# Index scores woven into a unit's products, own places for four query units, smaller first loads from two queues

## The reference

```python
h = rms_norm(x, norm_g)
proj = h @ w_in            # q, k, v, gate_a, u_b, gate_b, q_idx, k_idx, w_idx, merge
q, k = rope(rms_norm(q)), rope(rms_norm(k)); q_idx, k_idx = rope(q_idx), rope(k_idx)
s = einsum('bqhd,bkd->bqhk', q_idx, k_idx)               # index scores, 8 heads
score = einsum('bqhk,bqh->bqk', relu(s), w_idx * scale)
sel = top_k(where(visible, score, -inf), 128)            # keys each query may see
attn = softmax over the selected keys of q k^T, times v
y_a = (attn * silu(gate_a)) @ w_a;  y_b = (pool(u_b) * silu(gate_b)) @ w_b
x = x + (sigmoid(m_a) * y_a + sigmoid(m_b) * y_b) @ w_out
```

## Time and profile before

| | |
|---|---|
| median of 3 runs | 1560.16 us (1555.54, 1560.16, 1560.35) |
| the profiled execution | 1556.19 us, span 1554.3 us |
| PE busy | 1499.2 us, 96% |
| PEld, DVE, ACT, POOL busy | 1208.8, 952.0, 550.9, 971.3 us |
| mean granted TensorE clock | 0.994 |
| read from HBM | 116.02 MB, 76 GB/s over the span |

### The profile page before, as it was taken

The page is one execution under the profiler, slowest core; times in us unless marked ns, Lnnn a source line. Parts: engine busy times, 40 slices in busy tenths (PEclk is TensorE's granted clock), DMA queues, the critical chain, the costliest instruction groups (busy, mean ns, idle before and its releaser), DMA issues.

```text
span 1554.3 us, 24339 instructions
## 1 busy us (share of the span) xinstructions
PE 1499.2 (96%) x8516; PEld 1208.8 (78%) x8516; DVE 952.0 (61%) x2033; ACT 550.9 (35%) x1280; POOL 971.3 (62%) x1496
## 2 busy tenths in 40 slices
PE   7999999999999999999999999999998999999999
PEld 7776547678778778877989888889996877777777
DVE  6874781567676640046777788944448789894251
ACT  4446682333333310044564333341125523333100
POOL 6533415656565688776886644546888774455685
PEclk9999999999999999999999999999999999999999
DMA  7210001222222332332222211112222221121223
GB/s 257 66 48 28 28 1 46 77 71 93 93 94 94 94 104 88 96 98 77 89 69 82 69 55 55 55 55 76 95 82 70 87 88 49 48 68 55 68 95 108
DMA packets 37774, 119.42 MB, mean 77 GB/s; under 512 B 5424, under 2 KB 7600, under 8 KB 37424
## 3 DMA queue, kind: packets, MB, share of 16 engines
q1 hardware_dynamic: 36544, 116.06, 23.3%
q10 hardware_dynamic: 1136, 2.09, 0.4%
HBM read 116.02 MB, written 2.10 MB: 76 GB/s over the span
## 4 chain that ended last, share of the span: by engine, by line
PE 79%; DVE 11%; ACT 3%; POOL 3%; issue 3%; DMA 1%; SPq 0%; POOLq 0%; ACTq 0%; DVEq 0%
PE ps L778 62%; PE ps L1240 3%; PE ps L797 2%; PE ps L791 2%; PE ps L980 2%; PE ps L902 2%; POOL wlo L645 2%; PE ps L1315 1%; DVE score L2385 1%; POOL whi L641 1%; DVE score L2384 1%; PE ps L1310 1%; ACT pts L1539 1%; DVE probs L2403 1%; PE ps L1290 1%
## 5 line engine op out<-in xcount | busy, mean ns | idle before, releaser
L778 PE MATMUL ps<-hh,whi 128*128 128x512 f32 (+1 forms) x1448 | 511.4, 353 | 5.3 <-DVE hl L2177 1.7
L778 PE MATMUL ps<-hl,whi 128*128 128x512 f32 (+1 forms) x1448 | 502.8, 347 | 0.0
L778 PE MATMUL ps<-hh,wlo 128*128 128x512 f32 (+1 forms) x1448 | 501.5, 346 | 0.0
L641 POOL TENSOR_SCALAR whi<-raw 128x256 fp32r<-128x256 f32 x564 | 257.8, 485 | 332.9 <-PE ps L778 331.4
L645 POOL TENSOR_TENSOR wlo<-raw,whi 128x256 fp32r<-128x256 f32 x564 | 442.7, 816 | 11.8
L778 PEld LDWEIGHTS ps<-hh,whi 128*128 128x128 f32 x1448 | 273.9, 189 | 59.4 <-issue 11.3
L778 PEld LDWEIGHTS ps<-hh,wlo 128*128 128x128 f32 x1448 | 274.1, 189 | 34.9
L778 PEld LDWEIGHTS ps<-hl,whi 128*128 128x128 f32 x1448 | 274.0, 189 | 33.0 <-issue 0.7
L735 POOL TENSOR_TENSOR wlo<-raw,whi 128x256 fp32r<-128x256 f32 x160 | 134.7, 873 | 92.8 <-ACT whi L1586 92.8
L1959 DVE TENSOR_TENSOR tmp<-tmp 128x512 f32<-128x512 f32 x12 | 10.8, 900 | 118.3 <-ACT tmp L1624 90.0
L778 PE MATMUL ps<-plain_high,whi 128*128 128x264 f32 (+2 forms) x232 | 74.0, 319 | 6.6 <-POOL wlo L645 6.2
(11 more groups left out here) (363 smaller groups left out, 2709.9 us busy)
## 6 DMA issues: line engine op xcount, KB each, us to landing
raw<-in_w SPq DMA_DIRECT2D x197, 512.0 KB, 3.5
raw<-in_w SPq DMA_DIRECT2D x8, 256.0 KB, 3.4
x<-in_x SPq DMA_DIRECT2D x4, 512.0 KB, 8.1
out<-x SPq DMA_DIRECT2D x8, 256.0 KB, 4.4
raw<-in_w SPq DMA_DIRECT2D x12, 128.0 KB, 2.9
raw<-in_w SPq DMA_DIRECT2D x4, 384.0 KB, 3.4
cw_k<-in_cw1k SPq DMA_DIRECT2D x1, 1024.0 KB, 5.5
cw_v<-in_cw1v SPq DMA_DIRECT2D x1, 1024.0 KB, 7.4
```

The source lines that it names most:

```text
L641: ins = pool.tensor_scalar(whi[s][:, c:c + PIECE], raw[s][:, c:c + PIECE], 1.0, 0.0, ALU.mult, ALU.add)
L778: mm = pe.matmul(out, lhs, rhs, start=start and n == 0, stop=stop and n == 2)
```

## The change

1. `lunit` takes a list `between` of index calls: the first goes ahead of the unit, the others into its matmul stream at equal distances. In a slot with index scores the last unit is taken out of the spacers and computed so, behind the rest; ACT does the relus before that unit's eviction. In the first hybrid layer mg8 moves from slot 10 to slot 9, in the second mg6 from slot 6 to slot 5; the order of units stays.
2. `QUERY_EXTRA` has four units a layer: QI0 and Q1 in `query_high` and `query_low`, QI1 and Q0 in the two halves of `bh` and `bl`, which are not in use then. QI2, QI3, Q2 and Q3 take the two common places. POOL's order of units is the same.
3. The first loads come in pieces of 2, 2 and 4 chunks for the three value units, on SP; the gate weights, the gains, x chunks 0 and 1 (one each) and the pair 2, 3 are issued by ACT. The splits follow the pieces; the last pieces of ACT and DVE stand one turn later.
4. The root is spread behind chunk 6, group 2.

```diff
-        QUERY_EXTRA = [U_LAYER + l * L_UNITS + 2 for l in range(LAYERS)]
+        QUERY_EXTRA = {U_LAYER + l * L_UNITS + 2 + c: spot for l in range(LAYERS)
+                       for c, spot in ((0, 0), (1, 1), (4, 2), (5, 0))}
...
+                spot = QUERY_EXTRA[n]
+                if spot:
+                    col = (spot - 1) * D + k * P
+                    return (bl if low else bh)[:].rearrange("p k t -> p (k t)")[:, col:col + count * P]
...
-                units = ["mg0 mg1", "gb0", "ub0 mg2", "mg3", "gb1 mg4", "ub1", "mg5", "gb2 mg6", "ub2", "mg7", "gb3 mg8",
+                units = ["mg0 mg1", "gb0", "ub0 mg2", "mg3", "gb1 mg4", "ub1", "mg5", "gb2 mg6", "ub2", "mg7 mg8", "gb3",
...
-                units = ["gb0", "ub0", "mg4", "gb1", "ub1", "mg5", "mg6 gb2", "ub2", "mg7", "mg8 gb3", "ub3", "mg9",
+                units = ["gb0", "ub0", "mg4", "gb1", "ub1", "mg5 mg6", "gb2", "ub2", "mg7", "mg8 gb3", "ub3", "mg9",
...
-            sp.dma_start(raw[0][:, 0:HALF], io["w"][FIRST[0]][:, 0:HALF]).then_inc(*tick("half_in0", 0, 16))
-            sp.dma_start(wg[:], io["wg"]).then_inc(*tick("wg_in", 0, 16))
-            sp.dma_start(raw[1][:, 0:HALF], io["w"][FIRST[1]][:, 0:HALF]).then_inc(*tick("half_in1", 1, 16))
-            sp.dma_start(raw_third[:, 0:HALF], io["w"][FIRST[2]][:, 0:HALF]).then_inc(*tick("half_in2", 2, 16))
-            sp.dma_start(vec[:], io["vec"]).then_inc(*tick("vec_in", 0, 16))
-            x_pair(0)
+            sp.dma_start(raw[0][:, 0:PIECE], io["w"][FIRST[0]][:, 0:PIECE]).then_inc(*tick("quarter_in0", 0, 16))
+            sp.dma_start(raw[1][:, 0:PIECE], io["w"][FIRST[1]][:, 0:PIECE]).then_inc(*tick("quarter_in1", 1, 16))
+            sp.dma_start(raw_third[:, 0:PIECE], io["w"][FIRST[2]][:, 0:PIECE]).then_inc(*tick("quarter_in2", 2, 16))
+            sp.dma_start(raw[0][:, PIECE:HALF], io["w"][FIRST[0]][:, PIECE:HALF]).then_inc(*tick("half_in0", 0, 16))
...
-            for c in range(1, 4):
+            for c in range(2, 4):
                 x_pair(c)
...
-            for half in range(2):
-                first_half(half)
-                third_half(half)
+            for k0, count in ((0, PIECE), (PIECE, PIECE), (HALF, HALF)):
+                first_piece(k0, count)
+                third_piece(k0, count)
...
+            for l in range(LAYERS):
+                first = U_LAYER + l * L_UNITS
+                n = first + 2
                 for s in range(2):
-                    split(n // 2 - 1, s, False)
+                    split(first // 2, s, False)
                 if l:
                     pool.wait_ge(*at("gated_a", (l - 1, plans[l - 1]["slots"] - 1)))
                 split_extra(n)
-                split(n // 2, 1, False)
-                with pool.Fori(n // 2 + 1, (n + L_UNITS) // 2 - 1) as i:
+                pool.wait_ge(ty.sem("unit_used"), unit_ready(first))
+                split_extra(n + 1)
+                for s in range(2):
+                    split(n // 2 + 1, s, False, unit_ready(first + s))
+                split_extra(n + 4)
+                pool.wait_ge(ty.sem("unit_used"), unit_ready(n))
+                split_extra(n + 5)
+                for s in range(2):
+                    split(n // 2 + 3, s, False, unit_ready(n + 2 + s))
+                with pool.Fori(n // 2 + 4, (first + L_UNITS) // 2) as i:
...
-                    if (k, t) == (7, 0):
+                    if (k, t) == (6, 2):
                         spread_root("pre")
...
-                def lunit(m, out, free=(None, None), half=None):
+                def lunit(m, out, free=(None, None), half=None, between=()):
 
+                    if between:
+                        index(*between[0])
                     high, low = weights_of(m)
+                    spans = cols2(l) if half is None or half[1] != "ub" else [(0, TH), (TH, TH)]
+                    stops = {i * len(spans) * DC // len(between): between[i] for i in range(1, len(between))}
...
                         for k in range(DC):
+                            if tok * DC + k in stops:
+                                index(*stops[tok * DC + k])
...
+                    indices = [what for kind, what in plan["side"][s] if kind == "index"]
+                    woven = spacers.pop() if indices else None
...
-                    for kind, what in plan["side"][s]:
-                        if kind == "index":
-                            index(*what)
                     for f in spacers:
                         fill(f)
+                    if woven:
+                        fill(woven, indices)
...
+            act.dma_start(wg[:], io["wg"]).then_inc(*tick("wg_in", 0, 16))
+            act.dma_start(vec[:], io["vec"]).then_inc(*tick("vec_in", 0, 16))
+            for k in range(2):
+                act.dma_start(x[:, k, META:T], io["x"][:, k, :]).then_inc(*tick(f"x_one{k}", 0, 16))
+            act.dma_start(x[:, 2:4, META:T], io["x"][:, 2:4, :]).then_inc(*tick("x_in1", 0, 16))
...
                 if c == 0:
-                    second_low(1)
+                    second_low(PIECE, PIECE)
+                if c == 1:
+                    second_low(HALF, HALF)
```

More of the change, by code:

```diff
@@ L679, in split_first, with first_piece, third_piece @@
                 ins.then_inc(ty.sem("unit_split"), 1)
-            def first_half(half):
-                pool.wait_ge(*(at("raw_in0", 0) if half else at("half_in0", 0)))
-                for c in range(half * HALF, half * HALF + HALF, PIECE):
+            def first_piece(k0, count):
+                pool.wait_ge(*({0: at("quarter_in0", 0), 2: at("half_in0", 0), 4: at("raw_in0", 0)}[k0]))
+                for c in range(k0, k0 + count, PIECE):
                     ins = pool.tensor_scalar(wvh[:, c:c + PIECE, 0:P], raw[0][:, c:c + PIECE], 1.0, 0.0, ALU.mult, ALU.add)
                 ins.then_inc(ty.sem("unit_high"), 1)
-                pool.wait_ge(ty.sem("unit_high"), half + 1)
-                for c in range(half * HALF, half * HALF + HALF, PIECE):
+                pool.wait_ge(ty.sem("unit_high"), k0 // PIECE + 1)
+                for c in range(k0, k0 + count, PIECE):
                     ins = pool.tensor_tensor(wvl[:, c:c + PIECE, 0:P], raw[0][:, c:c + PIECE],
                                              wvh[:, c:c + PIECE, 0:P].bitcast(F32), ALU.subtract)
-                if half:
+                if k0 == HALF:
                     ins.then_inc(ty.sem("unit_split"), 1)
[L694 to L699, removed]
+            def third_piece(k0, count):
+                pool.wait_ge(*at("head_high", ("value", 2, k0)))
+                if k0 == HALF:
+                    pool.wait_ge(*at("head_low", ("value", 1, k0)))
+                for c in range(k0, k0 + count, PIECE):
                     ins = pool.tensor_tensor(wvl[:, c:c + PIECE, 2 * P:3 * P], raw_third[:, c:c + PIECE],
                                              wvh[:, c:c + PIECE, 2 * P:3 * P].bitcast(F32), ALU.subtract)
-                    if half:
+                    if k0 == HALF:
                         ins.then_inc(ty.sem("unit_split"), 1)
@@ L835, in _ @@
             for k in range(DC):
[L836 to L837 removed]
+                if k in (0, PIECE, HALF):
+                    pe.wait_ge(*at("head_low", ("value", 1, k)))
                 pe.wait_ge(*at("head_low", k))
@@ L1164, in qunit @@
                         for k in range(DC):
-                            if c == 0:
-                                mm = unit_extra(QUERY_EXTRA[l], out[:, tok, 0:n], k, plain_high[:, k, lo:lo + n],
+                            if place(l, L_QI + c) in QUERY_EXTRA:
+                                mm = unit_extra(place(l, L_QI + c), out[:, tok, 0:n], k, plain_high[:, k, lo:lo + n],
                                                 plain_low[:, k, lo:lo + n])
@@ L1211, in squares_of, with fill @@
                     mm.then_inc(*tick("q_squares", (l, c)))
-                def fill(f):
+                def fill(f, between=()):
                     nonlocal g_free
@@ L1229, in fill @@
                         else:
-                            lunit(unit_of(kind, c), G[:, mine[0]:mine[-1] + 1], [g_free[b] for b in mine], (l, kind, c))
+                            lunit(unit_of(kind, c), G[:, mine[0]:mine[-1] + 1], [g_free[b] for b in mine], (l, kind, c), between)
                         for tok, b in enumerate(mine):
@@ L1893, in _ @@
                         exped2(s + 2)
-                    for kind, what in plan["side"][s]:
-                        if kind == "index":
-                            index(*what)
                     for f in spacers:
                         fill(f)
+                    for what in indices:
+                        index(*what)
+                    if woven:
+                        fill(woven)
                 a_high(plan["slots"] - 2)
@@ L1986, in _, with second_low @@
                 .then_inc(*tick("head_low", ("gate", 1)))
-            def second_low(half):
-                ks = slice(half * HALF, half * HALF + HALF)
```

(8 more changed lines are left out.)

32 lines of the change are left out of this document (18 added, 14 removed).

## The result

| | before | changed |
|---|---|---|
| median of 12 runs | 1558.67 us | 1568.38 us |
| lowest and highest | 1555.49, 1563.53 | 1561.15, 1570.09 |
| profiled execution, span | 1556.19, 1554.3 | 1568.31, 1566.5 |
| mean granted clock of the profiled execution | 0.994 | 0.984 |

The ratio is 1.0055, with a 95% interval of 1.004 to 1.007: 8.6 us slower by the ratio (9.7 by the medians). 1545 had been forecast.

A forecast was written before the change was run, and what follows sets the result against it. PE was taken to bound the kernel, with work in 96% of the span. Terms 2.0 - 1.0 + 7.9 + 4.1 = 13.0 us off 1556.19 gave 1543.2; half of 4.0 us added made 1545, own range 1540 to 1550.

The forecast's parts named there:

- The sum: Whole kernel: 2.0 for first loads, -1.0 for query unit places, 7.9 and 4.1 for the hybrid layers, 13.0 us gained.
- the head: Kernel start: first loads in pieces, x lands sooner, root spread sooner; 2.0 us faster, bounds 0 and 3.5.
- the weave: Hybrid layers' slots: index score pairs put into unit products; 7.9 us faster in the first layer, 4.1 in the second.
- The rival with the clock: Query stretches: PE idles 4 to 5 us twice, two new low stretches at 3.4 us each; 1552, chance 0.12.
- the slower case: Hybrid slots: PE waits for DVE in many, each dropping the clock at 3.4 us; 1565, chance 0.03.
- Places: Query stretches: POOL waits go, waits for rotated queries grow to 4.2 and 4.8 us; 0.5 us loss a layer, 1.0 total.
- the 3 us by which DVE was said to lead PE where it is least: First hybrid layer: DVE's estimated smallest lead over PE, which was to swallow 3.3 us of PE's gain.
- The first layer: First hybrid layer: 6.8 us gained by slot 9, plus 1.1 from DVE's own shorter chain; 7.9 us faster.
- The second: Second hybrid layer: DVE starts 2.8 us earlier in slot 0 and gains 1.3 in slots 5 and 6; 4.1 us faster.
- The wait for bh: First hybrid layer, slot 9: mg8 moves, DVE's 1.91 us wait goes, woven scores end 0.8 later; 1.1 us gained.
- Both low stretches behind the 400-column groups: Behind index groups of 400 columns: half-clock stretches taken as gone, worth 2.4 and 3.4 us.
- DVE's score waits: Slots 10 to 13, then 4 to 9 of the second layer: new PE waits for DVE, 3 to 4 us in all.

The follow-up runs named there:

- e5_keep_warm2: The changed kernel plus idle PE products in both query waits and in slot 12 (first hybrid layer) and slot 8 (second): 1559.15 us, ratio 0.9982 to before.
- e7_places_warm: The kernel before plus only the places for four query units and 18 idle products ahead of each QI3 rotation wait: 1558.72 us, ratio 0.999.
- e6_weave_warm: The kernel before plus only the woven index scores and 13 idle products in slot 12 (first hybrid layer) and slot 8 (second): 1551.05 us, ratio 0.9934.
- e10_weave_units2: The kernel before plus woven index scores, later units moved into slots 11, 7 and 8, and mg6 ahead of gb2: 1540.06 us, ratio 0.9887.
- e8_head_load: The kernel before plus only the head's part, with unit 4's load issued ahead of the compression weights: 1560.76 us, ratio 1.0003.
- e4_keep_warm: The changed kernel plus idle products in both query waits and, one slot too late, in slots 13 and 9: 1569.70 us, ratio 1.0066 to before.
- e3_weave: The kernel before plus only the woven index scores, with mg8 and mg6 moved: 1554.65 us, ratio 0.9983.
- e12_all: The changed kernel plus unit 4's load earlier, early index scores one unit later, moved units, and mg6 ahead of gb2: 1536.34 us, ratio 0.9855 to before.

## Why the prediction was wrong, step by step

**The step that failed: what a wait costs.** The sum priced each wait by its length alone. Five times (the head, both query stretches, slot 12 of the first hybrid layer and slot 8 of the second) the change put one wait of 3.9 to 5.2 us where no wait had been over 2.8 (but the very first), and each time the clock halved for 3.4 to 6.8 us. The time missed 1545 by 23 us; 9 to 11 of them are the clock in four of these places (`e5_keep_warm2`). The other large terms are the head and the weave, below: even with the clock kept there the kernel took 1559.15 us, 9 above the range. The rival with the clock had 1552 and 0.12 for two such places, and the slower case named DVE's waits as the mechanism, but had it need over four of them and gave it 0.03. The Trainium skill (TensorE: Matmul & The Clock Gate, section Why this matters for your kernels) warns of idle gaps that drop the clock to half rate. The trace agrees: `e5_keep_warm2` has the same lateness of DVE and no such gap in four of the five places, and is 9 us faster.

**Places.** Forecast 1.0 slower, measured 5.3. The waits themselves came out: 4.8 and 5.2 us against 4.2 and 4.8, and 0.7 us a layer by POOL beside DVE against 0.5. What the sum left out is 2.3 and 2.2 us of clock, and with the clock kept (`e7_places_warm`) the part lies between nothing and 3 us faster, near the forecast.

**The head.** Forecast 2.0 faster, measured 5.3 slower. The first product came at 9.12 (8.5), and DVE's last sum ended 1.9 earlier (2.0), at 23.88. The term that was mis-sized is POOL's: unit 3's load 2.3 us late and not 1.3, unit 4's load behind 2.1 MB, which I had not followed, and unit 4's split 5.6 us and not 4.4, now that it lies beside DVE's norm. So unit 4 was ready at 34.05, not 31.2, and a wait of 4.2 us brought the clock down: 3.4 us late where 2.0 early was forecast. The other 1.9 of the 5.3 are likely low stretches in the first block.

**The weave.** Forecast 12.0 faster; measured 2.7, and where the clock was kept in slots 12 and 8 (`e6_weave_warm`) 10.3 by its ratio, 8.4 by the medians and 7.5 in the two hybrid layers of its profile. In the profile its lag behind before, at the same product of PE (start in it, start in before), goes so:

| place | lag, us |
|---|---|
| ahead of the slots (779.12 against 774.04) | 5.1 |
| behind slot 0 (862.06, 857.91) | 4.2 |
| behind slot 4 (924.16, 924.94) | -0.8 |
| behind slot 7's wait (936.98, 934.96) | 2.0 |
| behind slot 9 (979.15, 979.95) | -0.8 |
| end of the first hybrid layer (1156.68, 1154.94) | 1.7 |
| behind slot 8's wait in the second (1382.56, 1384.96) | -2.4 |

So PE gained what it was to gain: 0.9 and 4.9 us in slots 0 and 4 (1.3 and 5.5 forecast), 2.8 in slot 9. It gave 2.8 back in slot 7 and 2.5 around slot 12. The step that failed is the 3 us by which DVE was said to lead PE where it is least. In slot 7 that lead was nothing: before, ACT waited 4.50 us there for the pooled products, and PE met its eviction just in time.

```profile
928.72 0.39 ACT L1810 ACTIVATE merge<-ps 128x264 f32<-128x264 f32 x1 [4.50 <-DVE merge L2463]
```

DVE had gained 3.3 us by then (1.8 behind before) and not the 6.8 that were forecast, so PE waited. `e10_weave_units2`, which puts mg6 into that wait, confirms it. The first layer gave 3.3 us against 7.9. The second gave 4.1 against 4.1, but by luck: DVE gained 4.3 us around slot 0 (2.8 forecast) and nothing that lasted in slots 5 and 6 (1.3).

In slot 9 the forecast was off by less. DVE in slot 9 of the first, in order of time:

```profile
956.96 0.76 DVE L2384 TENSOR_SCALAR score<-relu,v 128x528 f32<-128x528 f32 x1 [3.74 <-ACT relu L1834]
...
959.71 1.64 DVE L2387 SCALAR_TENSOR_TENSOR score<-relu,v,score 128x528 f32<-128x528 f32 x2 [0.83 <-ACT relu L1834]
962.46 1.64 DVE L2387 SCALAR_TENSOR_TENSOR score<-relu,v,score 128x528 f32<-128x528 f32 x2 [1.12 <-ACT relu L1834]
965.24 1.64 DVE L2387 SCALAR_TENSOR_TENSOR score<-relu,v,score 128x528 f32<-128x528 f32 x2 [1.13 <-ACT relu L1834]
```

Before, the seven additions had followed each other in 6.54 us. Woven, a pair comes every 2.75 us and DVE needs 1.64, so it idles 3.1 us within the group; its part ends 2.5 us later and not 0.8. The wait for bh that goes gives 2.9 back and not 1.9, so DVE gains 0.3 us there where 1.1 was forecast: weaving took from DVE in this slot most of what it gave to PE. The gap of 3.7 us ahead of the group stayed as well.

**What was right.** Both low stretches behind the 400-column groups and all relu waits of the groups went; the second layer's slot 0 holds one wait of 1.2 us (about 1 forecast); DVE's score waits came in slots 12 and 8, within the slots named, though with 8.1 us in all they are twice the 3 to 4 forecast.

**What stays open.** The low stretches at 104, 128 and 193 us lie in work that the change doesn't touch. They are not its doing alone, for `e6_weave_warm` has them with the first block and the head of before, the first as:

```profile
100.65:107.48 6.83, 6.83 (x31) 4.95 (x30) 2.83 (x11) 3.38 (x12) 0.76 (x2) 0.50 0.25 79
```

They cost the changed kernel's profile 5.5 us. They come and go between executions of one kernel: the 12 runs of `e5_keep_warm2` go from 1553.47 us at a mean clock of 0.998 to 1561.55 at 0.991. Before's profile is a clean one: its mean clock is 0.994, that of the 29 runs beside `e5` to `e8` is 0.991 on average, an estimate of some 8 us more at the lower level. All six profiles with the changed head show such stretches there, and two of eight with the old one, which points at the head; but over whole runs the mean clock of `e8_head_load` (0.990 in 12 runs) is hardly below before's 0.991. Whether the head makes them likelier isn't settled.

## What to carry to other kernels

Do not price a wait by its length alone. Here each gap of about 4 us or more brought up to 3.4 us of lost clock on top, gaps of 1 to 2 us mostly nothing; so an edit that removes small waits must be followed to where they gather, and that place be filled, with real work if the order allows (in the weave it was worth some 7 us more than idle products at an equal mean clock). And when one engine is made faster, look for the first place where it meets the others with nothing to spare: here slot 7, where the profile of before showed no wait of PE, only one of ACT for DVE. When work is spread to feed one engine evenly, ask what the spacing does to the engine behind it.

## What the runs showed of the hardware

Idle products of 128 columns in a wait kept the clock at 1.00 in all four places tried. Every wait of 3.9 us or more other than the very first (for `wg`) had a low stretch around or just behind its end: 14 waits in six profiles. The one of 2.82 in slot 7 had one of 3.4 us in two of six profiles (`e4_keep_warm`, `e5_keep_warm2`), and waits of 1.8 to 2.0 us for POOL had one now and then (`e3_weave` at 1196, `e8_head_load` at 788, `e10_weave_units2` at 782, `e12_all` at 33). A long wait is not the only occasion: at 104.46 us in the changed kernel and at 848.46 in `e7_places_warm` a low stretch began with no wait of PE over 0.8 us in the 10 us ahead. The scatter of one kernel's runs, up to 10.8 us here, goes with the mean clock: about 1.1 us for each 0.001 (12 runs of `e5_keep_warm2`, 29 of before beside them).
